# Moved waits in the FFN of a hybrid decoder layer: two late weight loads, two silus, one sum, and the order of the last norms

## Chip, cores and metric

One Trainium2 chip, one core, one launch. The metric is the device time in microseconds (us); the median of several runs is compared. TensorE is called PE, VectorE DVE, ScalarE ACT, GpSimd POOL; SP is the queue that issues all the DMAs named here.

## The reference

One decoder layer over x of 1024 rows by 1024 columns in float32. The first half (three kinds of attention, an output projection, a norm and a residual) is not touched by the change. The second half is

```
h = rms_norm(x, ln_ffn_pre)
f = (silu(h @ ffn_w_gate) * (h @ ffn_w_up)) @ ffn_w_down     # D_FF = 2816
x = x + rms_norm(f, ln_ffn_post)
```

## The kernel before

**Products.** The FFN is written as block products with sums of blocks as operands, seven in place of eight, all of 512 columns. Each float32 operand is cut into a high and a low part, and a product is three matmuls for each block of 128 (high by high, high by low, low by high). The list `seq` (made by `plan_products`) holds 238 products, numbered s. Steps 0 to 155 belong to 22 units u of the gate and up projection with the kinds P1, P2, P6, P7, P5, P3, P4, each of 12 matmuls. The first steps are P1 and P2 of the units 0 to 3 (s = 0 to 7), then P6, P7, P5 of unit 0 (8, 9, 10), P2 of unit 4 (11), P3 and P4 of unit 0 (12, 13), P6 of unit 1 (14). Steps 152, 154 and 156 to 237 are the down projection: three rounds c over 3, 4 and 4 pairs of units, seven kinds D2, D1, D6, D7, D4, D5, D3 in that order, and four output tiles m in each kind. A product of round 0 has 9 matmuls, one of the rounds 1 and 2 has 12. In round 0, D7 has the steps 166 to 169, D5 174 to 177, D3 178 to 181; D2 of round 1 has 182 to 185. D3 of round 2 has 234 to 237, the last.

**Queues.** Every engine runs its instructions strictly in the order written. ACT and DVE walk through the steps s, and at s they cut the stationary operand of step s + 6 (`cut_hi` on ACT, L2057, then `cut_lo` on DVE, L2292). PE waits with step s for its `cut_lo`. ACT copies a half-finished PSUM bank away (`snap_first`, `snap_second` L2070, `snap_third`), and DVE's `first_block(u)` (L2298) adds P2's bank to the copy of P1. `silu_first(u)` (L2078) waits for `first_block(u)`. In `product`, a P2 of unit u from 2 up waits until `first_block(u - 2)` is done, since it takes the same bank: `pe.wait_ge(c11_done, u - 1)`. P5 of unit u waits for `snap_second(u)`, and `snap_second(0)` itself for the last of the ten cuts of the transposed activations (`top_rest`, L2287). `block_sums(1)` is four DVE sums of weights for unit 1, written behind `cut_lo(12)` at step 6. Up to the first steps of the loop, ACT and DVE follow an order written out by hand (called the prologue here).

**Down projection.** DVE makes the sums of the down weights (`down_sums`, L2273 to L2281) at steps from `plan_sums`; ACT (`block_hi_cut`, L2106) and DVE (`block_lo_cut`, L2330) cut them at steps from `plan_blocks`. The cut of the D7 sums stands at steps 162, 163, 164 and the D7 sums at 161, 162, 163. At each step DVE writes: cuts of blocks, then `add_out` (L2325, adds the bank to the running output; a later product that takes the bank waits for it), then `cut_lo(s + 6)`, then sums of weights. SP issues, in the order of a sorted list: `load_acts(q)` (L1890, the activations of round-and-kind q, into `f_stage` for even q and `f_scr` for odd q), `load_late_gate` (L1906, 512 KB each, waits for a D3 sum of the round before), `load_pair_up` (L1898, 512 KB each), the loads for the tail and the stores. q = 6 is D3 of round 0, q = 7 is D2 of round 1.

**Tail.** For an output tile t the class `Finish` has ACT square both halves (`square`, L2615), POOL multiply one half by the gain (`apply_gain`, L2620), and for t from 4 up DVE multiply the other half (`gain_late`, L2628) once that half is squared. ACT makes the mean (L2646), POOL the root (`root`, L2656), DVE the normed residual (`norm`, L2672, both halves; `norm_half`, L2681, one), and SP stores it. They stand behind the last eight `add_out`.

Of the kernel before, what the change touches and what calls it, by code (L numbers as in the profile page):

```python
# [1616 lines left out]
def plan_sums(place):  # L1617


    end, sums = place["P4", UNITS - 1, 0] + 1, []  # L1620
    for k in range(PAIR_SIZES[0]):
        sums += [(end - 1 + k, 0, kind, k) for kind in ("D5", "D6")]
        sums += [(place["D6", 0, 0] - 1 + k, 0, "D7", k), (place["D7", 0, 0] + 2 + k, 0, "D3", k)]
    for c in range(1, PAIR_CHUNKS):
        first = place["D4", c - 1, 0]
        made = [(kind, k) for kind in ("D5", "D6", "D7", "D3") for k in range(PAIR_SIZES[c])]
        sums += [(first + 3 * i // 2, c, kind, k) for i, (kind, k) in enumerate(made)]
    return sorted(sums, key=lambda x: x[0])


def out_and_ffn(nc, core, x, x1, w_gate, w_up, w_pairs, act_pairs, keep, mem, fin):
# [124 lines left out]
    def wait_taken(eng, kind, c, m):  # L1756

        if (kind, c) in COPIED:
            eng.wait_ge(y_copied, copied_at[kind, c, m] + 1)
        else:  # L1760
            eng.wait_ge(y_added, added_at[kind, c, m] + 1)
# [40 lines left out]
    def ahead_of(s):  # L1802

        held = at("P7", 1)
        if s == at("P5", 0):
            return (held, s + AHEAD)
        return (s + AHEAD,) if 3 < s < NS - AHEAD and s + AHEAD != held else ()
# [42 lines left out]
    def sp_program(sp):  # L1850
# [68 lines left out]
        for t in range(NT):  # L1919
# [10 lines left out]
            elif t == NT - 1:  # L1930
# [16 lines left out]
        order += [(NU - 21 if q == 0 else NU - 7.3 if q == 1 else cut_of(q - 2) + 0.7, load_acts, (q,)) for q in range(rounds)]  # L1947
        order += [(at("P5", UNITS - 1) + 0.1 + 0.1 * k if c == 0 else NU + 2 + 0.1 * k if c == 1 else place["D4", c - 2, 0] + 0.1 * k, load_pair_up, (c, k))
                  for c in range(PAIR_CHUNKS) for k in range(PAIR_SIZES[c])]
        order += [(place["D7", c - 1, 0] + 0.1 * k, load_late_gate, (c, k)) for c in range(1, PAIR_CHUNKS) for k in range(PAIR_SIZES[c])]  # L1950
        order += [(place["D1", LAST_ROUND, 0] + 0.1 * t if t < 2 else place["D4", LAST_ROUND, 0] + 0.1 * t, load_last, (t,)) for t in range(NT)]
        for _, what, args in sorted(order, key=lambda job: job[0]):
            what(*args)
        for t in range(NT - 2):
            fin.store(sp, t)
        fin.store_halves(sp, NT - 2)
        fin.store_halves(sp, NT - 1)
        sp.wait_ge(fin.out_done, 16 * (NT + 2))
        for u in range(2):
            sp.wait_ge(x1_out[u], 16 * (NT // 2))  # L1960

# [36 lines left out]
    def act_program(act):  # L1998
# [34 lines left out]
        def top_cut(i):  # L2033
            j, what = TOP_PARTS[i]
            act.wait_ge(y_done, NT)
            act.wait_ge(top_sum, SUMS_AT[j][TOP_NEEDS[what]])
            act.copy(top_part(topH, j, what), top_part(QT, j, what)).then_inc(top_hi, 1)

        def cut_hi(s):
            kind, u, m = seq[s]  # L2040
            if kind in S_STEP:
                act.wait_ge(s_done, 4 * u + S_STEP[kind])
            elif paired(s):
                act.wait_ge(act_in[round_of(s) % 2], acts_in(round_of(s)))
            else:
                wait_raw(act, raw_index(s))
            if s >= W_RING:
                act.wait_ge(prod_done, s - W_RING + 1)
            elif s >= 2:
                act.wait_ge(y_done, NT)  # L2050
                if s >= 5:
                    act.wait_ge(y_normed, NT)
                if s >= 6:
                    act.wait_ge(xn_done, NT)
                if s >= 7:
                    act.wait_ge(xT_done, NT)
            act.copy(slot_part(s, 0), source(s)).then_inc(hi_done, 1)  # L2057

        def snap_first(u):
            act.wait_ge(prod_done, at("P1", u) + 1)  # L2060
            if u >= 3:
                act.wait_ge(a0_done, u - 2)
            elif u == 2:
                act.wait_ge(squares, 2 * NT)
            act.copy(p1_room(u)[:], ps[:, X_BANK[u % 4], :]).then_inc(p1_done, 1)
# [10 lines left out]
        def silu_first(u):  # L2076
            act.wait_ge(c11_done, u + 1)
            act.activation(p1_room(u)[:], p1_room(u)[:], ACT.Silu).then_inc(s11_done, 1)  # L2078
# [52 lines left out]
        block_hi(NT - 1)  # L2131
        top_cut(3)
        snap_first(1)
        top_cut(4)
        cut_hi(6)
        top_cut(5)
        cut_hi(7)
        silu_first(0)
        cut_hi(8)
        top_cut(6)  # L2140
# [2 lines left out]
        cut_hi(9)  # L2143
        top_cut(8)
        top_cut(9)
        silu_first(1)

        for s in range(NS):
            kind, u, m = seq[s]
            for at_step, n in cuts:  # L2150
                if at_step == s:
                    block_hi_cut(n)
            if kind == "P1" and u > FIRST_DRAWN:
                snap_first(u)
            elif kind == "P6":
                snap_second(u)
            elif kind == "P5":
                snap_third(u)
            elif kind == "P3":
                silu_second(u)  # L2160
            elif (kind, u) in COPIED and s >= NU:
                if s == NU:
                    copy_out(place["D2", 0, 0])
                    copy_out(place["D2", 0, 1])
                copy_out(s)
            for v in (3, 4):
                if s == at("P4", v - 3) + 1:
                    snap_first(v)
                elif s == at("P4", v - 3) + 2:
                    silu_first(v)  # L2170
            if s == at("P1", FIRST_DRAWN + 1) + 2:
                silu_first(FIRST_DRAWN + 1)
            if s and seq[s - 1][0] == "P2" and (seq[s - 1][1] == 2 or seq[s - 1][1] > FIRST_DRAWN + 1):
                silu_first(seq[s - 1][1])
            for n in ahead_of(s):
                cut_hi(n)
            if finished(s):
                if finished(s) == (0, 0):
                    wait_up_read(act, LAST_ROUND - 1)
                wait_taken(act, kind, u, m)  # L2180
                fin.square(act, *finished(s))
                if finished(s)[0] >= M_PAIRS and finished(s)[1] == 0:
                    fin.mean(act, finished(s)[0])

    def dve_program(dve):
# [108 lines left out]
        def first_block(u):  # L2294

            dve.wait_ge(prod_done, at("P2", u) + 1)
            dve.wait_ge(p1_done, u + 1)
            dve.tensor_tensor(p1_room(u)[:], ps[:, Y_BANK[u % 2], :], p1_room(u)[:], ALU.add).then_inc(c11_done, 1)  # L2298
# [84 lines left out]
        for s in range(NS):  # L2383
            kind, u, m = seq[s]
            for at_step, n in cuts:
                if at_step == s:
                    block_lo_cut(n)
            if s and seq[s - 1][0] == "P5":
                last_block(seq[s - 1][1])
            for v in (3, 4):  # L2390
                if s == at("P4", v - 3) + 1:
                    first_block(v)
            if s == at("P1", FIRST_DRAWN + 1) + 1:
                first_block(FIRST_DRAWN + 1)
            if kind == "P2" and (u == 2 or u > FIRST_DRAWN + 1):
                first_block(u)
            if s and seq[s - 1][0] == "P3":
                late_half(seq[s - 1][1])
            if kind == "P4":
                early_half(u)  # L2400
            if paired(s) and (kind, u) not in COPIED:
                add_out(s)
            for n in ahead_of(s):
                cut_lo(n)
                if seq[n][0] == "P3" and seq[n][1] + 1 < UNITS:
                    block_sums(seq[n][1] + 1)
            for at_step, *item in sum_plan:
                if at_step == s:
                    down_sums(*item)
            if paired(s) and u == LAST_ROUND:  # L2410
                n = s - place["D5", LAST_ROUND, 0]
                if n == 0:
                    fin.first_means(dve)
                elif 1 <= n < 4:
                    fin.norm(dve, n - 1)
                elif n == 4:
                    fin.half_means(dve)
                    wait_taken(dve, *seq[s])
                    fin.gain_late(dve, 4)
                    fin.norm(dve, 3)  # L2420
                elif n in (5, 6):
                    wait_taken(dve, *seq[s])
                    fin.gain_late(dve, n)
                    fin.norm(dve, n - 1)
                    if n == 6:
                        fin.norm_half(dve, 6, 1)
        fin.norm_half(dve, NT - 2, 0)
        wait_taken(dve, *seq[NS - 1])
        fin.gain_late(dve, NT - 1)
        fin.norm_half(dve, NT - 1, 1)  # L2430
# [127 lines left out]
class Finish:  # L2558
# [42 lines left out]
    def store_halves(self, sp, t):  # L2601
        for n, i in enumerate((1, 0)):
            cols = slice(i * HALF, (i + 1) * HALF)
            sp.wait_ge(self.sum_done, t + (t == NT - 1) + 1 + n)
            sp.dma_start(self.out[t * P:(t + 1) * P, cols], self.room(t)[:, cols]).then_inc(self.out_done, 16)

    def constants(self, pool):
# [231 lines left out]
```

## Time and profile before

| | |
|---|---|
| median of 3 runs | 1252.41 us (1250.11 to 1258.15) |
| the profiled execution | 1252.77 us, span 1251.0 us |
| PE busy | 1217.7 us, 97% |
| DVE busy | 866.4 us, 69% |
| ACT busy | 605.7 us, 48% |
| POOL busy | 181.4 us, 15% |
| mean granted clock of PE | 0.993 |
| 640 to 1000 us | PE busy 360.00 us with 1590 matmuls, 0.226 us each; 12 of them take 2.7 us, 9 take 2.04 |
| busy share of the DMA engines | 0.00 from 626 to 640 us; 0.00 from 1059 to 1062; 0.62 from 1062 to 1067; 0.86 from 1067 to 1083 |

Times in the rows are us from the span's start. In a timeline row the first number is the start, the second the busy time, and a bracket tells how long the engine was idle just before and what released it. Rows of one engine lie a little over each other, so the pace is read from start to start: on DVE 0.60 us for an operation whose busy time is 0.69, and 1.20 for one of 1.28. "issue" is a wait that the profile ascribes to nothing.

### The profile page before, as it was taken

Reading aid. Unit: us, or ns where it says so; the run is one execution under the profiler, and the core shown is the slowest. Engines: PE = TensorE matmul, PEld = TensorE weight load, DVE = VectorE, ACT = ScalarE, POOL = GpSimd, SP = SyncE. Lnnn points to the kernel's source line nnn. Section 1 sums busy time; section 2 is a strip of 40 time slices with the busy share of each in tenths; the row PEclk is TensorE's granted clock in tenths of the full one; section 3 lists DMA queues with packets and bytes.
Section 4 is the critical chain, followed back from the end, with each engine's and each line's share of the span. In section 5 each row is a group of like instructions: output and inputs, shape, how many; then the busy total and the mean of one; then the engine's idle time right before and its main releaser. Section 6 shows DMA issues by size and latency. Waiting matters only on the chain.

```text
span 1251.0 us, 18763 instructions
## 1 busy us (share of the span) xinstructions
PE 1217.7 (97%) x6592; PEld 1042.2 (83%) x6592; DVE 866.4 (69%) x1641; ACT 605.7 (48%) x1167; POOL 181.4 (15%) x153
## 2 busy tenths in 40 slices
PE   9999999999999999999989999999999999999996
PEld 7898878888988999888878888888888888788885
DVE  6323788858878665355876657667666568897888
ACT  5432677657776566344653333333333345444343
POOL 5230111111000000011001112112122021000114
PEclk9999999999999999999999999999999999999998
DMA  6303511136842100222312232333332455743443
GB/s 234 120 1 119 118 37 49 35 110 158 182 121 77 26 18 18 68 101 100 119 42 100 94 125 67 103 127 103 108 105 72 144 193 195 259 156 115 151 169 135
DMA packets 66881, 136.93 MB, mean 109 GB/s; under 512 B 8503, under 2 KB 27199, under 8 KB 66788
## 3 DMA queue, kind: packets, MB, share of 16 engines
q1 hardware_dynamic: 66788, 135.74, 34.0%
q8 instruction: 53, 0.87, 0.3%
q14 instruction: 40, 0.33, 0.1%
HBM read 90.33 MB, written 28.60 MB: 95 GB/s over the span
## 4 chain that ended last, share of the span: by engine, by line
PE 79%; DVE 9%; issue 5%; ACT 3%; DMA 2%; SPq 1%; DVEq 0%; POOL 0%; ACTq 0%; POOLq 0%
PE ps L2506 32%; PE ps L2536 11%; PE ps L1097 7%; PE ps L2450 6%; PE ps L941 4%; PE ps L1077 4%; PE ps L886 3%; PE ps L960 3%; PE ps L1042 2%; PE ps L1050 2%; DVE ring L1468 2%; PE ps L975 1%; DMA m_qs<-m_qn 1%; DVE ring L1460 1%; DVE QT L2325 1%
## 5 line engine op out<-in xcount | busy, mean ns | idle before, releaser
L2506 PE MATMUL ps<-f_topH,f_W 128*128 128x512 f32 x704 | 221.0, 389 | 3.8 <-DVE f_W L2292 2.1
L2506 PEld LDWEIGHTS ps<-f_topH,f_W 128*128 128x128 f32 x704 | 132.1, 188 | 32.0 <-DVE f_W L2292 4.6
L2292 DVE TENSOR_TENSOR f_W<-f_scr,f_W 128x512 fp32r<-128x512 f32 (+1 forms) x128 | 89.9, 705 | 84.9 <-ACT f_W L2057 84.8
L2506 PE MATMUL ps<-f_topL,f_W 128*128 128x512 f32 x352 | 136.9, 389 | 0.0
L1097 PE MATMUL ps<-V,m_tw 128*128 128x66 f32 (+1 forms) x1056 | 129.2, 273 | 2.3 <-DVE m_mix_n L1518 2.2
L1097 PEld LDWEIGHTS ps<-V,m_tw 128*128 128x128 f32 x1056 | 126.3, 193 | 5.3 <-DVE m_mix_n L1518 4.3
L2536 PE MATMUL ps<-f_headH,f_W 128*128 128x512 f32 x408 | 128.0, 390 | 2.2 <-issue 1.5
L2506 PE MATMUL ps<-f_headH,f_W 128*128 128x512 f32 x352 | 114.7, 390 | 0.0
L2536 PEld LDWEIGHTS ps<-f_headH,f_W 128*128 128x128 f32 x408 | 76.6, 188 | 19.6 <-issue 2.7
L2057 ACT CAST f_W<-f_scr 128x512 fp32r<-128x512 f32 (+1 forms) x128 | 77.6, 610 | 24.6 <-PE ps L2536 15.2
L2292 DVE TENSOR_TENSOR f_W<-ring,f_W 128x512 fp32r<-128x512 f32 x60 | 59.6, 1006 | 33.4 <-ACT f_W L2057 33.3
L1277 ACT COPY m_tw<-ps 128x512 f32<-128x512 f32 (+1 forms) x101 | 56.5, 568 | 52.0 <-PE ps L1097 29.8
L2536 PE MATMUL ps<-f_headL,f_W 128*128 128x512 f32 x204 | 79.4, 389 | 0.0
L2506 PEld LDWEIGHTS ps<-f_topL,f_W 128*128 128x128 f32 x352 | 66.1, 188 | 13.7
L2506 PEld LDWEIGHTS ps<-f_headH,f_W 128*128 128x128 f32 x352 | 66.1, 188 | 13.6
L2506 PE MATMUL ps<-f_headL,f_W 128*128 128x512 f32 x176 | 68.5, 389 | 0.0
L960 PE MATMUL ps<-m_hH,m_wH 128*128 128x512 f32 x144 | 60.4, 419 | 4.9 <-ACT QT L1178 4.8
L2536 PE MATMUL ps<-f_b22H,f_W 128*128 128x512 f32 x208 | 65.1, 389 | 0.0
L2450 PE MATMUL ps<-o_w,o_mH 128*128 128x512 f32 x224 | 60.5, 392 | 0.0
L2506 PE MATMUL ps<-f_b22H,f_W 128*128 128x512 f32 x176 | 57.8, 389 | 0.0
L2325 DVE TENSOR_TENSOR QT<-ps,QT 128x512 f32<-128x512 f32 x68 | 46.7, 687 | 15.7 <-PE ps L2536 15.7
L1042 PE MATMUL ps<-m_KSa,m_qs 128*128 128x256 f32 (+7 forms) x168 | 55.0, 345 | 2.3 <-DVE m_rows_sb L1475 1.2
(279 smaller groups left out, 2660.4 us busy)
## 6 DMA issues: line engine op xcount, KB each, us to landing
act_pairs<-QT SPq DMA_DIRECT2D x77, 256.0 KB, 4.1
m_qs<-m_qn SPq DMA_DIRECT2D x128, 128.0 KB, 2.4
ring<-in_ffn_w_up SPq DMA_DIRECT2D x22, 512.0 KB, 3.7
f_stage<-act_pairs SPq DMA_DIRECT2D x40, 256.0 KB, 3.6
ring<-in_ffn_w_gate SPq DMA_DIRECT2D x19, 512.0 KB, 4.5
f_scr<-act_pairs SPq DMA_DIRECT2D x37, 256.0 KB, 3.1
ring<-in_ffn_w_down SPq DMA_DIRECT2D x11, 512.0 KB, 5.3
f_pair_up<-in_ffn_w_down SPq DMA_DIRECT2D x11, 512.0 KB, 6.6
```

The source lines that it names most:

```text
L941: ins = pe.matmul(ps[:, b + a, 0:VW_HALF], h[:, k, tok], wv[:, w, k, a * VW_HALF:(a + 1) * VW_HALF], start=(k == 0 and h is hH and w == 0) ...
L960: ins = pe.matmul(ps[:, bank, :], w[:, n % W_ITEMS, cols], a[:, k, hf * HALF:(hf + 1) * HALF], start=(k == 0 and w is wH and a is hH), sto ...
L1042: pe.matmul(out, q_hi_, k, start=True, stop=False)
L1077: ins = pe.transpose(ps[:, bank, i * P:(i + 1) * P], rows, ident[:])
L1097: ins = pe.matmul(ps[:, SUMS, wide * i:wide * (i + 1)], tw[:, t % W_SLOTS, P * i:P * i + P], v, start=(kb == 0 and i == 0), stop=(kb == jo ...
L1277: act.copy(out, src).then_inc(kept_by["act"], 1)
L2057: act.copy(slot_part(s, 0), source(s)).then_inc(hi_done, 1)
L2292: dve.tensor_tensor(slot_part(s, 1), source(s), slot_part(s, 0).bitcast(F32), ALU.subtract).then_inc(lo_done, 1)
L2325: dve.tensor_tensor(part, product_, part, ALU.add).then_inc(y_added, 1)
L2450: ins = pe.matmul(ps[:, 2 * (t % 2) + hf, :], m[:, t % 2, k, :], w[k][:, a, hf * HALF:(hf + 1) * HALF], start=(k == 0 and m is mH and a == ...
L2506: ins = pe.matmul(ps[:, bank, :], whole[:, w, cols], halves[h][:, k0 + k, col:col + HALF], start=(begins and k == 0 and w == 0 and h == 0) ...
L2536: ins = pe.matmul(ps[:, bank, :], whole[:, w, k * P:(k + 1) * P], block(n)[h], start=(begins and k == 0 and w == 0 and h == 0), stop=(k == ...
```

## The change

It has five edits. (1) `load_late_gate` of round 1 moves behind `load_acts(6)` in SP's order. (2) In ACT's prologue `cut_hi(6)` and `cut_hi(7)` move ahead of `top_cut(4)`; `silu_first(1)` leaves the end of the prologue and `silu_first(2)` its place at step 6, and both now follow `snap_second(0)` at step 8. (3) On DVE `first_block(2)` moves from step 5 to step 8, behind `cut_lo(13)` and ahead of `cut_lo(14)`. (4) The D7 sums of round 0 are made one step earlier. (5) In the tail the steps 234, 235 and 236 run `norm` of the tile before and then `gain_late` of their own, without waiting in between; tile 6 is normed and stored whole, not in halves.

```diff
-        sums += [(place["D6", 0, 0] - 1 + k, 0, "D7", k), (place["D7", 0, 0] + 2 + k, 0, "D3", k)]
+        sums += [(place["D6", 0, 0] - 2 + k, 0, "D7", k), (place["D7", 0, 0] + 2 + k, 0, "D3", k)]
...
-        order += [(place["D7", c - 1, 0] + 0.1 * k, load_late_gate, (c, k)) for c in range(1, PAIR_CHUNKS) for k in range(PAIR_SIZES[c])]
+        order += [(place["D7", c - 1, 0] + 0.1 * k + (1.8 if c == 1 else 0), load_late_gate, (c, k)) for c in range(1, PAIR_CHUNKS) for k in range(PAIR_SIZES[c])]
...
-        for t in range(NT - 2):
+        for t in range(NT - 1):
             fin.store(sp, t)
-        fin.store_halves(sp, NT - 2)
         fin.store_halves(sp, NT - 1)
...
         snap_first(1)
+        cut_hi(6)
+        cut_hi(7)
         top_cut(4)
-        cut_hi(6)
         top_cut(5)
-        cut_hi(7)
         silu_first(0)
...
         top_cut(9)
-        silu_first(1)
...
-            if s and seq[s - 1][0] == "P2" and (seq[s - 1][1] == 2 or seq[s - 1][1] > FIRST_DRAWN + 1):
+            if s and seq[s - 1][0] == "P2" and seq[s - 1][1] > FIRST_DRAWN + 1:
                 silu_first(seq[s - 1][1])
+            if s == at("P6", 0):
+                silu_first(1)
+                silu_first(2)
...
-            if kind == "P2" and (u == 2 or u > FIRST_DRAWN + 1):
-                first_block(u)
+            if s == at("P6", 0) or kind == "P2" and u > FIRST_DRAWN + 1:
+                first_block(2 if kind == "P6" else u)
...
-                elif n == 4:
-                    fin.half_means(dve)
-                    wait_taken(dve, *seq[s])
-                    fin.gain_late(dve, 4)
-                    fin.norm(dve, 3)
-                elif n in (5, 6):
-                    wait_taken(dve, *seq[s])
-                    fin.gain_late(dve, n)
-                    fin.norm(dve, n - 1)
-                    if n == 6:
-                        fin.norm_half(dve, 6, 1)
-        fin.norm_half(dve, NT - 2, 0)
+                elif n >= 4:
+                    if n == 4:
+                        fin.half_means(dve)
+                    if n < 7:
+                        fin.norm(dve, n - 1)
+                        fin.gain_late(dve, n)
+        fin.norm(dve, NT - 2)
```

## Rows read from the trace of the kernel before

**Rows 1.** Who waited for whom, PE from 560 to 1251: total, times, longest us

```profile
PE ps L2506 <- DVE f_W L2292: 2.1, 1, 2.1
PE ps L2506 <- ACT QT L2070: 1.7, 1, 1.7
PE ps L2536 <- issue: 1.5, 1, 1.5
PE ps L2536 <- DVE f_headL L2330: 0.6, 1, 0.6
```

**Rows 2.** Timeline of PE, the first matmuls of P7, P5 and P2(4)

```profile
631.51 0.50 PE L2506 MATMUL ps<-f_topH,f_W 128*128 128x512 f32 x1 [2.13 <-DVE f_W L2292]
...
636.18 0.47 PE L2506 MATMUL ps<-f_topH,f_W 128*128 128x512 f32 x1 [1.66 <-ACT QT L2070]
...
639.02 0.39 PE L2506 MATMUL ps<-f_headH,f_W 128*128 128x512 f32 x1
```

**Rows 3.** Timeline of DVE: cut_lo 7 and 9, first_block(2), cut_lo 12 and 13

```profile
622.54 0.69 DVE L2292 TENSOR_TENSOR f_W<-f_gates,f_W 128x512 fp32r<-128x512 f32 x1 [0.66 <-ACT f_W L2057]
...
630.77 0.69 DVE L2292 TENSOR_TENSOR f_W<-f_scr,f_W 128x512 fp32r<-128x512 f32 x1
...
633.18 0.69 DVE L2298 TENSOR_TENSOR f_p1b<-ps,f_p1b 128x512 f32<-128x512 f32 x1
...
635.07 0.69 DVE L2292 TENSOR_TENSOR f_W<-f_scr,f_W 128x512 fp32r<-128x512 f32 x1 [0.60 <-ACT f_W L2057]
...
638.43 0.69 DVE L2292 TENSOR_TENSOR f_W<-ring,f_W 128x512 fp32r<-128x512 f32 x1
```

**Rows 4.** Timeline of ACT: cut_hi(6) and cut_hi(7)

```profile
619.32 0.62 ACT L2057 CAST f_W<-f_gates 128x512 fp32r<-128x512 f32 x1
...
621.89 0.62 ACT L2057 CAST f_W<-f_gates 128x512 fp32r<-128x512 f32 x1
```

**Rows 5.** Timeline of DVE: the third D7 cut, then add_out of step 174

```profile
1053.87 0.69 DVE L2330 TENSOR_TENSOR f_headL<-f_down_sums,f_headH 128x512 fp32r<-128x512 f32 x1 [0.69 <-ACT f_headH L2106]
...
1078.78 0.68 DVE L2325 TENSOR_TENSOR QT<-ps,QT 128x512 f32<-128x512 f32 x1
```

**Rows 6.** Timeline of PE: start of step 178, and the last matmul

```profile
1079.56 0.47 PE L2536 MATMUL ps<-f_headH,f_W 128*128 128x512 f32 x1 [1.49 <-issue]
...
1240.53 0.39 PE L2536 MATMUL ps<-f_b22H,f_W 128*128 128x512 f32 x1
```

**Rows 7.** Timeline of ACT: cut_hi(178) and cut_hi(182)

```profile
1075.43 0.51 ACT L2057 CAST f_W<-f_stage 128x384 fp32r<-128x384 f32 x1 [10.26 <-DMA f_stage<-act_pairs]
...
1082.97 0.62 ACT L2057 CAST f_W<-f_scr 128x512 fp32r<-128x512 f32 x1 [4.23 <-DMA f_scr<-act_pairs]
```

**Rows 8.** Timeline of SP's issues: late gates, acts 6, acts 7

```profile
1062.01 5.12 SPq L1906 DMA_DIRECT2D ring<-in_ffn_w_down  x4
1067.24 1.79 SPq L1890 DMA_DIRECT2D f_stage<-act_pairs  x3
...
1071.57 2.29 SPq L1890 DMA_DIRECT2D f_scr<-act_pairs  x4
```

**Rows 9.** Timeline of DVE in the tail: add_out(234), gain_late(5), add_out(237), the last halves

```profile
1233.89 0.68 DVE L2325 TENSOR_TENSOR QT<-ps,QT 128x512 f32<-128x512 f32 x1
...
1238.83 0.69 DVE L2628 TENSOR_TENSOR QT<-QT,e_last_gain 128x512 f32<-128x512 f32 x1 [0.89 <-ACT e_last_junk L2615]
...
1244.68 0.68 DVE L2325 TENSOR_TENSOR QT<-ps,QT 128x512 f32<-128x512 f32 x1
...
1247.10 0.75 DVE L2681 SCALAR_TENSOR_TENSOR e_xt_sums<-QT,e_rs,e_xt_sums 128x512 f32<-128x512 f32 x1 [0.48 <-POOL e_rs L2656]
1247.77 0.75 DVE L2681 SCALAR_TENSOR_TENSOR e_xt_sums<-e_gained_last,e_rs,e_xt_sums 128x512 f32<-128x512 f32 x1
```

**Rows 10.** By line: norm L2672 and root L2656, duration ns min/median/max, first to last

```profile
L2672 DVE SCALAR_TENSOR_TENSOR e_xt_up<-QT,e_rs,e_xt_up x4: 1277/1280/1714, 1232.3 to 1242.8; 128x1024 f32<-128x1024 f32 x4
...
L2656 POOL TENSOR_TENSOR e_rs<-e_ms,e_mhalf x4: 544/818/823, 1235.7 to 1246.5; 128x1 f32<-128x1 f32 x4
```

More of the change, by code:

```diff
@@ L1953, in sp_program @@
             what(*args)
-        for t in range(NT - 2):
+        for t in range(NT - 1):
             fin.store(sp, t)
-        fin.store_halves(sp, NT - 2)
         fin.store_halves(sp, NT - 1)
-        sp.wait_ge(fin.out_done, 16 * (NT + 2))
+        sp.wait_ge(fin.out_done, 16 * (NT + 1))
         for u in range(2):
@@ L2603, in store_halves @@
             cols = slice(i * HALF, (i + 1) * HALF)
-            sp.wait_ge(self.sum_done, t + (t == NT - 1) + 1 + n)
+            sp.wait_ge(self.sum_done, t + 1 + n)
             sp.dma_start(self.out[t * P:(t + 1) * P, cols], self.room(t)[:, cols]).then_inc(self.out_done, 16)
```

## The prediction, made before the changed kernel had run

> **What bounds the kernel now.** I read the busy shares first: PE works 97% of the span, so up to its end only PE's own pauses can be won. Then I read who PE waited for from the FFN on: four waits and no fifth, 2.1 + 1.7 + 1.5 + 0.6 = 5.9 us [rows 1]. Placing each in the timeline, the first two are P7 and P5 of unit 0 [rows 2], the one of 0.6 is the first D7 product of round 0, and the "issue" one is step 178, the first D3 product of round 0 [rows 6]. Last I read what follows PE's end: the last matmul is over at 1240.53 + 0.39 = 1240.9 [rows 6] and the span at 1251.0, so 10.1 us of tail hang on DVE. The change removes no matmul. It can win at most the pauses and a part of the tail.
>
> **Prologue and unit 0 (edits 2 and 3).** P7 waited for `cut_lo(9)`, which DVE reached at 630.77 [rows 3]. DVE had been busy since it waited 0.66 for the high part of weight 7 [rows 3], and that came late because ACT made it at 621.89, behind the top cuts; cut straight behind number 6, at 619.32 + 0.5, it is ready by 620.5 [rows 4]. So the 0.66 goes, `cut_lo(9)` starts at 630.1, and P7 at 630.85 instead of 631.51. Edit 2 costs no new work: cuts and silus are as many as before. The wait for weight 9 that is left, 2.13 - 0.66 = 1.5, is DVE being full.
>
> P5 waited until 636.18 for `snap_second(0)` [rows 2], which ACT reached late, behind two silus and four cuts. Without the silus it waits only for the last top cuts, some 1.8 us behind `cut_lo(9)`: about 632.0 for DVE and 632.5 for ACT. P7 takes 2.73 us, so P5 could start at 630.85 + 2.8 = 633.6, and its wait of 1.66 is gone.
>
> But look what is late next. P2 of unit 4 is the product behind P5 and waits for `first_block(2)`. Before, that ran at 633.18 [rows 3] and was long done. Now it stands behind `cut_lo(12)`, the four sums of `block_sums(1)` and `cut_lo(13)`. From `cut_lo(12)` to `cut_lo(13)` DVE took 638.43 - 635.07 = 3.36 us [rows 3], all of it those sums. In the new order `cut_lo(11)` takes the place of `first_block(2)`, 633.18 - 0.66 = 632.5; `cut_lo(12)` follows at 633.1 (ACT, rid of the silus, no longer keeps it waiting 0.60), `cut_lo(13)` at 636.5, `first_block(2)` at 637.1 to 637.8. P5 would let P2(4) start at 633.6 + 2.75 = 636.35. So a wait of about 1.4 us appears there, and P2(4) starts at 637.8 instead of 639.02 [rows 2]. **Gain 1.2 us**. If DVE also saves 0.2 in the handover of weight 6, it is 1.4. I take 1.3. The ends: 0 if the sums take longer, and 639.02 - 636.35 = 2.7 if `first_block(2)` isn't late. Behind the moved silus ACT holds `cut_hi(14)` and `snap_third(0)` until 638.4; step 14 is due three products (8 us) after step 11, and P3, which wants `snap_third(0)`, one product after it at 640.5. Both are covered.
>
> **D7 sums (edit 4).** D7 waited 0.6 for its third low cut, 1053.87 + 0.69 [rows 5]. There the two engines pass one step to and fro: ACT cuts a sum, copies a bank, cuts a weight; DVE cuts its low part, makes the next sum, and only that lets ACT go on (DVE idle 0.69 for ACT). With the sum made a step sooner ACT waits for none of them; it follows PE, and the third cut comes a product (2.04 us) sooner, against a need of 0.6. The sum of 0.60 now stands ahead of an `add_out` that is wanted 4 us later: nothing. **Gain 0.8**, the 0.63 idle and the slower first matmuls after a pause (0.50 instead of 0.39). Ends 0 and 0.8.
>
> **SP order (edit 1).** Step 178 seems to wait for nothing, but DVE's `add_out(174)` ran at 1078.78 [rows 5], and 178 uses its bank: 1079.46 against 1079.56 [rows 6]. DVE was late because `cut_lo(178)`, written ahead of it, waited for ACT, and ACT sat 10.26 us for `load_acts(6)` [rows 7]. SP issued that at 1067.24 behind four late gates that occupied it from 1062.01 [rows 8]. These wait for D3 sums, `load_acts(6)` only for `cut_lo(173)`, which ended at about 1059.4. In the new order it is issued there, while the DMA engines have nothing to do, and has 15 us. The late gates can't be issued before 1062.0 anyway, and `load_acts(6)` takes 1.8 us of SP: moving behind it costs them nothing. What is late next is `load_acts(7)`, for which ACT sat until 1082.97 [rows 7]. SP is free of 1.8 us ahead of it (1071.57 to about 1069.7 [rows 8]) and 0.75 MB less is queued, so it should land at about 1081. The `add_out` of step 177 stands 2.5 us behind `cut_hi(182)` and is wanted by step 181, at 1077.9 + 3 x 2.04 = 1084.0: just in time. **Gain 1.8**: the 1.49, the slow restart and about 0.2 of small gaps behind it. Ends: 0.8 if step 181 waits a microsecond, 2.1 if all small gaps go too.
>
> **Tail (edit 5).** DVE is the engine to follow from 1233.89 [rows 9]. Its work from there is four `add_out`, one small mean, four `norm`, four `gain_late` and two last halves (tile 6 in halves costs 0.1 more). It waited 0.89 for the square ahead of `gain_late(5)`, as much ahead of `gain_late(6)`, 0.3 ahead of `gain_late(4)`, and 0.48 for the last root [rows 9]; the first three waits came from `gain_late(n)` standing straight behind `add_out(n)`. In the new order a `norm`, paced at 1.20 us [rows 10], lies between, and square, mean and root fit beside the DVE work of one step (0.6 + 1.2 + 0.6 = 2.4 us). From 1233.89 `add_out(237)` then has ahead of it three `add_out`, the mean, three `norm` and three gains: 3 x 0.60 + 0.6 + 3 x 1.20 + 3 x 0.60 = 7.8, so it starts at 1241.7 (PE is done at 1240.9, so not earlier for PE's sake) instead of 1244.68. From there square, mean and root of tile 7 took 1247.10 - 1244.68 = 2.4 us with a root of 0.54; other roots took 0.82 [rows 10], so 2.4 to 2.7, and the first of the last halves starts at 1244.1 to 1244.4 instead of 1247.10. `norm(6)` and the last gain (1.8) fit inside. The last two halves and their store come as before. Storing tile 6 whole puts 512 KB on the queue 1 us ahead of them; it was the same bytes before. **Gain 2.7**, ends 1.5 and 3.0.
>
> The roots are where a page speaks against this. The last root took 0.54 us beside an idle DVE, the others up to 0.82 beside a busy one, and the slowest `norm` of the group 1.71 beside POOL's gains, against 1.28 [rows 10]. The Trainium skill, "SBUF — State Buffer", section "SBUF: two separate sides", says that a DVE operation with two SBUF inputs and a GpSimd operation that reads SBUF exclude each other for a whole instruction. The rows agree in direction. By that rule a root could sit out a whole `norm` now that DVE has no pauses, which would take 1.2 from the tail's gain.
>
> **Sum.** 1.3 + 0.8 + 1.8 + 2.7 = 6.6 us against the profiled execution's 1252.77 (span 1251.0 and 1.8 around it): 1246.2. That execution lies 0.4 above the median of 1252.41, far inside the runs' spread of 8 us, so I leave it: **1246.2 us**.
>
> **Rivals.**
> (a) `first_block(2)` is not late, everything comes at its upper end: 2.7 + 0.8 + 2.1 + 3.0 = 8.6, 1244.2. For it: both big waits of unit 0 are named by the profile. Against: the 3.36 us of sums. Chance 0.15.
> (b) The waits move instead of going: the roots sit out a `norm` (tail 1.5), step 181 waits (0.8), unit 0 gives 0.5: 3.6, 1249.2. Chance 0.20.
> (c) The change does nothing that can be seen, the time falls in the runs' own spread: 1251 to 1254. It needs PE to be paced by something that I don't see; the long stretches of full PE speak against it. Chance 0.08.
> (d) Slower: `first_block(2)` at step 8. Every microsecond that it comes after 637.8 is one on PE, as P2(4), then P3 and P4 wait in line. It turns unit 0 to a loss from 639.0 on, and the whole change only after 637.8 + 6.6 = 644.4, that is, if `block_sums(1)` took three times its 3.36 us, say, waiting for its weights. At 10 us more it gives 1256. Against: the DMA engines moved nothing from 626 to 640 us, so those weights had landed. Chance 0.05; by over 1%, 0.02.
> The forecast itself, 1245 to 1248: 0.52.
>
> **Range and chances.** 1243.0 to 1251.0 holds (a), the forecast and (b), and leaves out most of (c) and (d). Over 1% (12.5 us, about what a measurement of this kernel can tell from no change) is more than all four waits and the gain in the tail together, so "faster" gets 0.03, "slower" 0.02 and "same" 0.95.
>
> **What would show it.** P7 of unit 0 starts near 630.9 with some 1.5 us idle, P5 without a wait, P2(4) near 637.8 behind a wait for DVE L2298. No wait at the first D7 and D3 product of round 0; ACT idle far under 10 us at `cut_hi(178)`. `add_out(237)` about 0.9 us behind the last matmul instead of 3.8. I am wrong on unit 0 if P2(4) doesn't wait, on SP's order if step 181 or 182 waits over 1 us for `f_scr`, and on the tail if DVE idles for POOL ahead of a `norm`.

## The result and the profile after

The changed kernel took **1246.23 us** (median of 9 runs, 1244.60 to 1248.10), the kernel before 1251.46 us in 9 runs beside them (1248.59 to 1258.15): **ratio 0.995, 95% interval 0.9932 to 0.9968**. A second session gave 0.994 (0.9927 to 0.9952). The profiled execution took 1246.82 us with a span of 1245.0, against 1252.77 and 1251.0. No work went: PE still runs 6592 matmuls.

Who waited for whom, PE from 560 us to the end, in the changed kernel (total, times, longest). Two waits are left where [rows 1] had four, and one of them is new:

```profile
PE ps L2502 <- DVE f_p1b L2299: 1.3, 1, 1.3
PE ps L2502 <- DVE f_W L2293: 1.3, 1, 1.3
```

Lines have moved by a few: PE's products are L2502 and L2532 now, `cut_lo` L2293, `first_block` L2299, `add_out` L2326, `cut_hi` L2056, `norm` L2668, `root` L2652.

Timeline of PE: the first FFN matmul, P7, P2 of unit 4, step 178 and the last matmul, which answer to [rows 2, 6].

```profile
604.65 0.48 PE L2502 MATMUL ps<-f_headH,f_W 128*128 128x512 f32 x1
...
631.57 0.50 PE L2502 MATMUL ps<-f_topH,f_W 128*128 128x512 f32 x1 [1.29 <-DVE f_W L2293]
...
638.63 0.47 PE L2502 MATMUL ps<-f_headH,f_W 128*128 128x512 f32 x1 [1.33 <-DVE f_p1b L2299]
...
1076.64 0.39 PE L2532 MATMUL ps<-f_headH,f_W 128*128 128x512 f32 x1
...
1237.10 0.39 PE L2532 MATMUL ps<-f_b22H,f_W 128*128 128x512 f32 x1
```

P5 is not in the list of waits: its 1.66 is gone. But `first_block(2)` now keeps P2(4) waiting 1.33. Absolute times mislead here. The FFN began at 604.65 in this execution and at 603.75 in that of before, in code that is the same in both, so each stretch has to be read from its own start:

| stretch | before | after | gain | predicted |
|---|---|---|---|---|
| first FFN matmul to P2(4) | 35.27 | 33.98 | 1.29 | 1.3 |
| P2(4) to the last matmul's start | 601.51 | 598.47 | 3.04 | 0.8 + 1.8 |
| last matmul's start to the end | 10.47 | 7.90 | 2.57 | 2.7 |
| sum of the three | 647.25 | 640.35 | 6.90 | 6.6 |
| start of the span to the first FFN matmul | 603.75 | 604.65 | -0.90 | 0 |

Timeline of DVE: `cut_lo(9)`, `cut_lo(12)`, `cut_lo(13)`, `first_block(2)`, which answer to [rows 3].

```profile
630.84 0.68 DVE L2293 TENSOR_TENSOR f_W<-f_scr,f_W 128x512 fp32r<-128x512 f32 x1
...
633.85 0.68 DVE L2293 TENSOR_TENSOR f_W<-f_scr,f_W 128x512 fp32r<-128x512 f32 x1
...
637.20 0.69 DVE L2293 TENSOR_TENSOR f_W<-ring,f_W 128x512 fp32r<-128x512 f32 x1
637.80 0.68 DVE L2299 TENSOR_TENSOR f_p1b<-ps,f_p1b 128x512 f32<-128x512 f32 x1
```

From 633.85 to 637.20, 3.35 us pass with `cut_lo(12)` and the four sums, as 3.36 before; `first_block(2)` ends at 638.48 and P2(4) starts at 638.63.

SP's issues (`load_acts(6)`, late gates, `load_pair_up`, `load_acts(7)`), which answer to [rows 8], and then ACT's `cut_hi(178)` and `cut_hi(182)`, which answer to [rows 7]:

```profile
1058.06 1.27 SPq L1890 DMA_DIRECT2D f_stage<-act_pairs  x3
1060.75 5.31 SPq L1906 DMA_DIRECT2D ring<-in_ffn_w_down  x4
1066.18 2.35 SPq L1898 DMA_DIRECT2D f_pair_up<-in_ffn_w_down  x4
1068.62 2.43 SPq L1890 DMA_DIRECT2D f_scr<-act_pairs  x4
```

```profile
1063.81 0.51 ACT L2056 CAST f_W<-f_stage 128x384 fp32r<-128x384 f32 x1
...
1079.55 0.62 ACT L2056 CAST f_W<-f_scr 128x512 fp32r<-128x512 f32 x1 [9.25 <-DMA f_scr<-act_pairs]
```

`cut_hi(178)` no longer waits. ACT's long pause has only moved: it now sits 9.25 us at `cut_hi(182)`, the next load (4.23 before), where little hangs on it. Idle time of ACT is not PE's.

Timeline of DVE in the tail: `add_out` of 234 and 237 and the two last halves, which answer to [rows 9]; then the root by line (ns min/median/max), which answers to [rows 10].

```profile
1230.47 0.68 DVE L2326 TENSOR_TENSOR QT<-ps,QT 128x512 f32<-128x512 f32 x1
...
1238.24 0.68 DVE L2326 TENSOR_TENSOR QT<-ps,QT 128x512 f32<-128x512 f32 x1
...
1241.15 0.75 DVE L2677 SCALAR_TENSOR_TENSOR e_xt_sums<-QT,e_rs,e_xt_sums 128x512 f32<-128x512 f32 x1 [0.44 <-POOL e_rs L2652]
1241.82 0.75 DVE L2677 SCALAR_TENSOR_TENSOR e_xt_sums<-e_gained_last,e_rs,e_xt_sums 128x512 f32<-128x512 f32 x1
```

```profile
L2652 POOL TENSOR_TENSOR e_rs<-e_ms,e_mhalf x4: 1011/1034/1037, 1232.3 to 1240.1; 128x1 f32<-128x1 f32 x4
```

From `add_out(234)` to `add_out(237)` DVE takes 7.77 us (7.8 predicted, 10.79 before) and never waits. All four roots take 1.01 to 1.04 us where they took 0.54 to 0.82.

### The profile page after: what moved, and what is told of

Its sections match the earlier page's. It is cut to its first block, busy times and chain, and to the rows that moved or that the text cites. A ratio compares the mean times of both kernels' runs of the same rounds, so it can differ in the third digit from the quotient of the medians.

```text
span 1245.0 us, 18759 instructions
## 1 busy us (share of the span) xinstructions
PE 1218.6 (98%) x6592; PEld 1044.3 (84%) x6592; DVE 864.8 (69%) x1640; ACT 605.6 (49%) x1167; POOL 182.1 (15%) x153
## 4 chain that ended last, share of the span: by engine, by line
PE 79%; DVE 10%; issue 4%; ACT 3%; DMA 2%; POOL 1%; SPq 1%; DVEq 0%; POOLq 0%; ACTq 0%
PE ps L2502 31%; PE ps L2532 14%; PE ps L1097 7%; PE ps L2446 4%; PE ps L941 4%; PE ps L1077 4%; PE ps L886 4%; PE ps L960 3%; PE ps L1042 2%; PE ps L1050 2%; DVE ring L1468 2%; PE ps L975 1%; DMA m_qs<-m_qn 1%; DVE ring L1460 1%; DVE m_rows_sb L1475 1%
## 5 line engine op out<-in xcount | busy, mean ns | idle before, releaser
L2502 PE MATMUL ps<-f_topH,f_W 128*128 128x512 f32 x704 | 220.7, 389 | 1.3 <-DVE f_W L2293 1.3
L2502 PEld LDWEIGHTS ps<-f_topH,f_W 128*128 128x128 f32 x704 | 132.1, 188 | 29.0 <-DVE f_W L2293 1.7
L2293 DVE TENSOR_TENSOR f_W<-f_scr,f_W 128x512 fp32r<-128x512 f32 (+1 forms) x128 | 89.8, 704 | 87.8 <-ACT f_W L2056 87.7
L2502 PE MATMUL ps<-f_topL,f_W 128*128 128x512 f32 x352 | 136.9, 389 | 0.0
L2532 PE MATMUL ps<-f_headH,f_W 128*128 128x512 f32 x408 | 127.3, 389 | 0.0
L2502 PE MATMUL ps<-f_headH,f_W 128*128 128x512 f32 x352 | 114.8, 390 | 1.3 <-DVE f_p1b L2299 1.3
L2056 ACT CAST f_W<-f_scr 128x512 fp32r<-128x512 f32 (+1 forms) x128 | 77.6, 610 | 27.5 <-PE ps L2532 15.1
L2532 PEld LDWEIGHTS ps<-f_headH,f_W 128*128 128x128 f32 x408 | 76.6, 188 | 16.3 <-issue 0.3
L2293 DVE TENSOR_TENSOR f_W<-ring,f_W 128x512 fp32r<-128x512 f32 x60 | 59.6, 1006 | 33.4 <-ACT f_W L2056 33.3
L2532 PE MATMUL ps<-f_headL,f_W 128*128 128x512 f32 x204 | 79.4, 389 | 0.0
L2502 PEld LDWEIGHTS ps<-f_headH,f_W 128*128 128x128 f32 x352 | 66.1, 188 | 15.3 <-DVE f_W L2293 1.7
L2502 PEld LDWEIGHTS ps<-f_topL,f_W 128*128 128x128 f32 x352 | 66.1, 188 | 13.8
L2502 PE MATMUL ps<-f_headL,f_W 128*128 128x512 f32 x176 | 68.5, 389 | 0.0
L2532 PE MATMUL ps<-f_b22H,f_W 128*128 128x512 f32 x208 | 65.2, 389 | 0.0
L2502 PE MATMUL ps<-f_b22H,f_W 128*128 128x512 f32 x176 | 57.7, 389 | 0.0
L2326 DVE TENSOR_TENSOR QT<-ps,QT 128x512 f32<-128x512 f32 x68 | 46.6, 685 | 15.8 <-PE ps L2532 15.8
```

Source lines behind the costliest of these rows:

```text
L2293: dve.tensor_tensor(slot_part(s, 1), source(s), slot_part(s, 0).bitcast(F32), ALU.subtract).then_inc(lo_done, 1)
L2502: ins = pe.matmul(ps[:, bank, :], whole[:, w, cols], halves[h][:, k0 + k, col:col + HALF], start=(begins and k == 0 and w == 0 and h == 0) ...
L2532: ins = pe.matmul(ps[:, bank, :], whole[:, w, k * P:(k + 1) * P], block(n)[h], start=(begins and k == 0 and w == 0 and h == 0), stop=(k == ...
```

## The experiments

All but the last two are single executions: they are told apart by stretches of the profile, not by the time of the whole. Each starts from the changed kernel. The columns: start of the first FFN matmul in the span; from there to P2(4); from P2(4) to the last matmul's start; from there to the end; span.

| kernel | FFN starts | to P2(4) | to last | tail | span |
|---|---|---|---|---|---|
| before | 603.75 | 35.27 | 601.51 | 10.47 | 1251.0 |
| changed | 604.65 | 33.98 | 598.47 | 7.90 | 1245.0 |
| block_early | 605.15 | 32.58 | 598.64 | 7.93 | 1244.3 |
| cuts_old | 603.29 | 34.82 | 598.67 | 7.92 | 1244.7 |
| split_sums | 605.71 | 33.27 | 598.21 | 7.91 | 1245.1 |
| sp_old | 601.42 | 34.05 | 600.63 | 7.90 | 1244.0 |
| d7_old | 606.99 | 34.16 | 599.23 | 7.92 | 1248.3 |
| tail_wait | 605.41 | 34.11 | 598.29 | 10.29 | 1248.1 |
| root_free | 601.89 | 33.95 | 598.68 | 8.38 | 1242.9 |
| tail_add_first | 606.02 | 33.92 | 598.30 | 7.96 | 1246.2 |

Where no edit touches a stretch, the rows differ by up to 0.24 us to P2(4), 0.47 from there to the last matmul and 0.03 in the tail; what is read as an effect lies above that. The spans would mislead: sp_old undoes a part of the change and has a smaller span than the changed kernel, because its FFN began 3.2 us sooner.

**block_early: is it `first_block(2)`?**

```diff
-            if s == at("P6", 0) or kind == "P2" and u > FIRST_DRAWN + 1:
-                first_block(2 if kind == "P6" else u)
+            if s == at("P1", 3) or kind == "P2" and u > FIRST_DRAWN + 1:
+                first_block(2 if kind == "P1" else u)
```

> Changed kernel, with first_block(2) moved to step 6, ahead of cut_lo(12) and the four sums of block_sums(1); the silus stay behind snap_second(0). My theory: P2 of unit 4 waits (1.33 us in the changed kernel) only because first_block(2) stands behind those sums. Then that wait is gone and P2(4) starts 1.3 to 1.5 us sooner after the first FFN matmul, 32.5 to 32.7 us instead of 33.98; P7 still waits 1.3. Rival: P2(4) is held by its own weight cut or by ACT, which sits in silu_first(2); then the wait stays at about 1.3 under another name.

P2(4) came at 32.58, 1.40 sooner, and its wait is gone. PE's timeline, P7 and P2(4):

```profile
632.14 0.50 PE L2502 MATMUL ps<-f_topH,f_W 128*128 128x512 f32 x1 [1.36 <-DVE f_W L2293]
...
637.73 0.39 PE L2502 MATMUL ps<-f_headH,f_W 128*128 128x512 f32 x1
```

That shows the place behind the sums to be the cause; the rival falls.

**cuts_old: what do the earlier cuts give?**

```diff
         snap_first(1)
-        cut_hi(6)
-        cut_hi(7)
         top_cut(4)
+        cut_hi(6)
         top_cut(5)
+        cut_hi(7)
```

> Changed kernel, with cut_hi(6) and cut_hi(7) back behind top_cut(4) and top_cut(5) on ACT. My theory: DVE is a full chain from weight 6 to first_block(2), and the 0.7 to 0.9 us that the earlier cuts gave runs through to P2(4): P7 starts 0.7 to 0.9 later (its wait is 2.0 to 2.2 instead of 1.3 to 1.4) and P2(4) starts at 34.6 to 34.9 us after the first FFN matmul instead of 33.98. Rival: P2(4) is paced by the sums' own waits, so only P7 moves, and P2(4) stays at 34.0.

P7's wait went from 1.29 to 2.13, and P2(4) came 0.84 later, with the same wait of its own. The two rows:

```profile
631.05 0.50 PE L2502 MATMUL ps<-f_topH,f_W 128*128 128x512 f32 x1 [2.13 <-DVE f_W L2293]
...
638.11 0.47 PE L2502 MATMUL ps<-f_headH,f_W 128*128 128x512 f32 x1 [1.33 <-DVE f_p1b L2299]
```

So DVE is one full chain from weight 6 to `first_block(2)`. Of the 1.29 us, 0.84 come from the cuts. The other 0.45 is what a subtraction leaves for the moved silus and `first_block(2)` together; no run put these two back, and rows of this stretch differ by 0.24. The place of `first_block(2)` alone gives away the 1.40 that block_early wins.

**split_sums: can P7's wait go too?**

```diff
-        sums(2, (2,))
-        sums(3, (2,))
+        sums(2, (3,))
+        sums(3, (3,))
         top_rest(6)
         top_rest(7)
         cut_lo(9)
+        sums(2, (4,))
+        sums(3, (4,))
+        cut_lo(10)
         top_rest(8)
...
         cut_hi(9)
+        cut_hi(10)
         top_cut(8)
```

Part 3 is the first of the two sums of part 2 and part 4 the second, with the counts that wait for them renumbered; `ahead_of` leaves out product 10. `first_block(2)` stands as in block_early.

> Changed kernel with first_block(2) at step 6 (as in block_early), and two of DVE's top sums, which only the last two top cuts need, moved behind cut_lo(9); cut_hi(10) and cut_lo(10) go ahead of those last top cuts. Theory: the 1.3 us that P7 still waits are DVE being full, and 1.2 us of it isn't needed by P7. Then P7 waits 0.1 to 0.3 us, P5 waits at most 0.6 for snap_second(0), and P2(4) starts 31.3 to 31.9 us after the first FFN matmul (32.58 in block_early, 33.98 in the changed kernel). Rival: the pause moves whole to P5, which needs those last top cuts by way of snap_second(0), and P2(4) stays at 32.6.

A miss: P2(4) at 33.27, later than the theory and the rival have it and 0.69 later than in block_early, though still 0.71 sooner than in the changed kernel. P7's wait fell only to 0.76, since the top cuts 6 and 7 on ACT now kept DVE waiting 0.57, and P5 got one of 1.03 for `snap_second(0)`, which the delayed top cuts and three weight cuts on ACT held up:

```profile
632.10 0.50 PE L2507 MATMUL ps<-f_topH,f_W 128*128 128x512 f32 x1 [0.76 <-DVE f_W L2295]
...
636.14 0.47 PE L2507 MATMUL ps<-f_topH,f_W 128*128 128x512 f32 x1 [1.03 <-ACT QT L2069]
```

P7's pause shrank by 0.60, and P5's new one is longer than that: 0.76 + 1.03 = 1.79 us where block_early has one wait of 1.36. The rival was nearer.

**sp_old: the order of two loads.**

```diff
-        order += [(place["D7", c - 1, 0] + 0.1 * k + (1.8 if c == 1 else 0), load_late_gate, (c, k)) for c in range(1, PAIR_CHUNKS) for k in range(PAIR_SIZES[c])]
+        order += [(place["D7", c - 1, 0] + 0.1 * k, load_late_gate, (c, k)) for c in range(1, PAIR_CHUNKS) for k in range(PAIR_SIZES[c])]
```

> Changed kernel, with the four late gates of round 1 back ahead of load_acts(6). My theory: the wait is made by the order in SP's queue. Then ACT sits some 10 us for f_stage again, add_out(174) comes late, and PE waits 1.3 to 1.7 us at step 178 under the name issue. Rival: the wait of before came from the D7 pause and the backlog it left on ACT and DVE, which is gone; then ACT waits for f_stage but PE shows no wait at step 178, and the stretch from P2(4) to the last matmul stays at 598.5 us.

P2(4) to the last matmul took 600.63, 2.16 more. ACT's row for `cut_hi(178)`, and PE's for step 178:

```profile
1070.98 0.51 ACT L2056 CAST f_W<-f_stage 128x384 fp32r<-128x384 f32 x1 [10.20 <-DMA f_stage<-act_pairs]
```

```profile
1075.11 0.47 PE L2532 MATMUL ps<-f_headH,f_W 128*128 128x512 f32 x1 [1.44 <-issue]
```

Here the D7 pause was absent and the wait came all the same: the order in SP's queue makes it. Behind it PE also starts the steps 179 and 181 late, by 0.25 and 0.29 us (0.25 and 0.27 in the kernel before); these gaps are too short for the list of waits.

**d7_old: the D7 sums one step later.**

```diff
-        sums += [(place["D6", 0, 0] - 2 + k, 0, "D7", k), (place["D7", 0, 0] + 2 + k, 0, "D3", k)]
+        sums += [(place["D6", 0, 0] - 1 + k, 0, "D7", k), (place["D7", 0, 0] + 2 + k, 0, "D3", k)]
```

> Changed kernel, with the D7 sums of round 0 back at the steps 161 to 163. My theory: ACT and DVE pass one step to and fro, so PE waits 0.5 to 0.7 us for the third D7 cut (DVE L2331) and that is all: P2(4) to the last matmul takes 0.8 us more than 598.5. Rival: with the other waits gone DVE has enough lead and no wait shows.

599.23, 0.76 more, with PE's wait of 0.6 (the first line) and the old rhythm of the D7 cuts on DVE, 2.75 us apart with 0.69 of waiting in each. In the changed kernel they are 1.67 and 1.07 apart, and the third one, at 1050.65, ends 2.2 us ahead of the matmul that needs it.

```profile
PE ps L2532 <- DVE f_headL L2331: 0.6, 1, 0.6
```

```profile
1053.34 0.69 DVE L2331 TENSOR_TENSOR f_headL<-f_down_sums,f_headH 128x512 fp32r<-128x512 f32 x1 [0.69 <-ACT f_headH L2105]
1056.08 0.69 DVE L2331 TENSOR_TENSOR f_headL<-f_down_sums,f_headH 128x512 fp32r<-128x512 f32 x1 [0.69 <-ACT f_headH L2105]
```

**tail_wait: the order of DVE or the whole tile?**

```diff
-                elif n >= 4:
+                elif n in (4, 5, 6):
                     if n == 4:
                         fin.half_means(dve)
-                    if n < 7:
-                        fin.norm(dve, n - 1)
-                        fin.gain_late(dve, n)
+                    wait_taken(dve, *seq[s])
+                    fin.gain_late(dve, n)
+                    fin.norm(dve, n - 1)
```

> Changed kernel, with gain_late(n) back straight behind add_out(n), ahead of norm(n-1), at the steps 234 to 236; tile 6 is still normed and stored whole. My theory: the order of DVE is the tail's gain. Then DVE waits 0.3, 0.9, 0.9 us for the squares again and from the last matmul's start to the end it takes 10.0 to 10.4 us instead of 7.9. Rival: the gain is the whole store and whole norm of tile 6; then it stays within 0.5 of 7.9.

10.29 us, with the three waits back (0.30 and twice 0.89):

```profile
1236.14 0.69 DVE L2624 TENSOR_TENSOR QT<-QT,e_last_gain 128x512 f32<-128x512 f32 x1 [0.89 <-ACT e_last_junk L2611]
...
1239.52 0.69 DVE L2624 TENSOR_TENSOR QT<-QT,e_last_gain 128x512 f32<-128x512 f32 x1 [0.89 <-ACT e_last_junk L2611]
```

So 2.39 of the tail's 2.57 us are the order. The 0.18 that is left goes, by subtraction, to the whole tile in place of two halves.

**root_free: who holds the root?**

```diff
-        fin.gain_late(dve, NT - 1)
         fin.norm_half(dve, NT - 1, 1)
+        fin.gain_late(dve, NT - 1)
         fin.norm_half(dve, NT - 1, 0)
...
         dve.wait_ge(self.rs_done, t - M_PAIRS + 2)
-        self.wait_gained(dve, t)
+        if i == 1:
+            dve.wait_ge(self.gained, 2 * M_PAIRS + t - M_PAIRS + 1)
+        else:
+            self.wait_gained(dve, t)
```

> Changed kernel, with the last gain on DVE (gain_late(7)) between the two last halves, so that DVE stands idle behind norm(6) while POOL makes the root of tile 7. It tests whether POOL's root is held by DVE's operation beside it. The roots took 1.01 to 1.04 us in the changed kernel, 0.54 for the one root of before beside an idle DVE. Theory (a root waits until DVE's operation with two SBUF inputs is over): the last root takes 0.5 to 0.65 us and the first last half starts 0.4 to 0.5 sooner after add_out(237) (2.9 us in the changed kernel), while the end stays within 0.2. Rival (the root simply takes 1.0 us when another operation of the queue precedes it closely): it still takes 1.0.

POOL's last two roots, the first beside a busy DVE and the second beside an idle one:

```profile
1235.10 1.03 POOL L2652 TENSOR_TENSOR e_rs<-e_ms,e_mhalf 128x1 f32<-128x1 f32 x1 [1.36 <-ACT e_ms L2642]
1237.49 0.55 POOL L2652 TENSOR_TENSOR e_rs<-e_ms,e_mhalf 128x1 f32<-128x1 f32 x1 [1.36 <-ACT e_ms L2642]
```

DVE's two last halves in the same kernel, with the gain between them:

```profile
1238.12 0.75 DVE L2680 SCALAR_TENSOR_TENSOR e_xt_sums<-QT,e_rs,e_xt_sums 128x512 f32<-128x512 f32 x1 [0.60 <-issue]
1238.79 0.68 DVE L2621 TENSOR_TENSOR e_gained_last<-QT,e_last_gain 128x512 f32<-128x512 f32 x1
1239.68 0.75 DVE L2680 SCALAR_TENSOR_TENSOR e_xt_sums<-e_gained_last,e_rs,e_xt_sums 128x512 f32<-128x512 f32 x1 [0.20 <-DVE e_gained_last L2621]
```

The root takes 0.55 us, and the first half starts 2.47 us behind `add_out(237)` instead of 2.91, as the theory has it. The end was missed: the gain now stands between the halves, with 0.20 of waiting for its own result behind it, and the tail is 8.38, 0.48 longer.

**tail_add_first: `add_out(237)` sooner.**

```diff
                     if n < 7:
                         fin.norm(dve, n - 1)
-                        fin.gain_late(dve, n)
+                    if n < 6:
+                        fin.gain_late(dve, n)
+                    elif n == 7:
+                        fin.gain_late(dve, 6)
```

> Changed kernel, with gain_late(6) behind add_out(237) instead of ahead of it. Theory: the tail is now the chain add_out(237), square, mean, root, two halves, and DVE has 0.44 us to spare inside it; add_out(237) 0.6 us sooner makes the tail 0.4 to 0.6 us shorter, 7.3 to 7.5 us from the last matmul's start to the end instead of 7.90. Rival: DVE's own work is the limit, nothing is won.

Nothing won: 7.96. `add_out(237)` did start 0.59 us sooner behind the last matmul. The rival has the reason: DVE's own work sets the end. Two waits of 0.20 for DVE's own results were added (`norm(6)` behind its gain, the first last half behind the last gain). The root now began inside `norm(6)` and took 1.32 us, but it was over at 1241.94, 0.41 us before the half that needs it started. DVE's `add_out(237)` and `norm(6)`, then POOL's last two roots:

```profile
1238.79 0.68 DVE L2326 TENSOR_TENSOR QT<-ps,QT 128x512 f32<-128x512 f32 x1
...
1240.26 1.28 DVE L2671 SCALAR_TENSOR_TENSOR e_xt_sums<-QT,e_rs,e_xt_sums 128x1024 f32<-128x1024 f32 x1 [0.20 <-DVE QT L2627]
```

```profile
1238.83 0.54 POOL L2655 TENSOR_TENSOR e_rs<-e_ms,e_mhalf 128x1 f32<-128x1 f32 x1 [1.36 <-ACT e_ms L2645]
1240.62 1.32 POOL L2655 TENSOR_TENSOR e_rs<-e_ms,e_mhalf 128x1 f32<-128x1 f32 x1 [1.25 <-ACT e_ms L2645]
```

These rows say what a root costs. By the pace of 1.20 us `norm(6)` ran until 1241.46, 0.84 us after the second root had begun, and the root took 0.48 more than that. The last root of the changed kernel fits the same sum: it began at 1240.08, 0.56 us before a gain was over, and took 1.04. So do the roots of 0.82 before, with 0.33 to 0.34 of a gain left. Over the twelve traces 45 of the 48 roots of the tiles 4 to 7 take 0.47 to 0.50 us more than the DVE operation beside them has left. Two others began when DVE's operation was over or within 0.02 us of its end, and took 0.55 and 0.54. The last one is the first root shown here: it began beside `add_out(237)`, with 0.56 us of it left, and took 0.54 all the same. That operation is as long as a gain but reads one of its two inputs from a PSUM bank (`ps`), where the gain and the `norm` read both from SBUF. So, as far as these traces show, a root sits out the rest of a DVE operation with two inputs in SBUF, and a DVE that is merely busy doesn't hold it; of the second half there is only this one case.

**block_early_timed and after_again.** The kernel of block_early and the changed kernel, both against the kernel before on one chip.

> The kernel of block_early, timed. By the stretches of the first look the part behind the first FFN matmul takes 639.2 us against 640.4 in the changed kernel and 647.3 in the one before. Theory: 1.2 us of PE's wait are gone for good, so it stands 8.1 us below the kernel before (ratio 0.9935) and 1.2 below the changed kernel. Rival: the start of the first FFN matmul, which moved between 601.4 and 607.0 us from execution to execution in code that no kernel here touches, covers the 1.2 us, and the two can't be told apart by their times.

> The changed kernel once more, on the same chip as block_early_timed. Expected ratio to the kernel before 0.994 to 0.996 (0.995 was measured). Its profile should again show two waits of PE in the FFN, 1.2 to 1.4 us each, and a tail of 7.9 us, with the first FFN matmul anywhere between 601 and 607 us and sooner where the granted clock of the first 600 us is higher.

block_early: 1243.19 us (1240.93 to 1244.72, 5 runs), before 1251.82 (9 runs), ratio 0.9935 (0.9921 to 0.9948). Changed kernel: 1243.72 us (1243.36 to 1245.53, 5 runs), ratio 0.994 (0.9927 to 0.9952). The FFN stretches took 638.92 and 640.21 us in their profiles, so the 1.3 us is there, and the changed kernel shows its two waits (1.34 and 1.33) and a tail of 7.89 again. Both ratios came as expected. But the medians of the two kernels lie 0.5 us apart and not 1.2, and the intervals overlap: as the rival has it, by the times alone block_early isn't shown to be faster than the changed kernel.

## Why the prediction was right

**Unit 0**: right in each step. P7's wait shrank (1.5 predicted, 1.29 measured), P5's vanished, and P2(4) got a new one of 1.33 (1.4 predicted) behind `first_block(2)`. The gain of 1.29 is what is left when one takes the two waits that vanish or shrink and looks for what is late next. Without a late `first_block(2)` the prediction had 2.7, its upper end, and block_early, where it isn't late, gives exactly that (35.27 - 32.58 = 2.69). The DVE handover that I priced at 0.66, with up to 0.2 more, gave 0.84. One reading was loose: the 3.36 us from `cut_lo(12)` to `cut_lo(13)` are not all sums. About 0.8 are `cut_lo(12)` itself and a short gap, and the four sums take 2.54; the forecast counted from start to start, so it doesn't suffer.

**D7 sums**: 0.8 predicted, 0.76 by d7_old. That ACT waits for none of these sums was nearly right: for the second and the third it still waits 0.15 us each, where it had been 1.23.

**SP order**: the mechanism was right and the term too small: 1.8 predicted, 2.16 by sp_old, 3.04 - 0.76 = 2.3 by the stretch. What I had too small were the gaps behind step 178: about 0.2 us in my sum, 0.25 at step 179 and 0.29 at step 181 in sp_old. (Rows of this stretch differ by 0.47 where nothing is edited, so the last tenths are not to be read.) `load_acts(7)` was in by 1079.55, 2.9 us behind the start of step 178 (1081 against 1077.9, 3.1 us, predicted), and left one gap of 0.15 us at step 181, the "just in time" of the prediction. block_early shows the same place once with 0.18.

**Tail**: 2.7 predicted, 2.57 measured. DVE's sum of work was right to 0.03 us. The part behind it was not: from `add_out(237)` to the first last half I allowed 2.4 to 2.7 us and it took 2.91, since the root took 1.04. The Trainium skill's rule of the shared port ("SBUF — State Buffer", section "SBUF: two separate sides") is what tail_add_first shows: the root waits for the rest of a DVE operation with two inputs in SBUF. The price I drew from it, a whole `norm` of 1.2, was too high for this order: the last root began beside a gain that had 0.56 us left. The price in my sum, a root of 0.54 to 0.82, was too low. The rival (b) falls, since the tail gave 2.57 and not 1.5, and (c) and (d) with the stretches.

**The median**: 1246.23 against 1246.2 is luck in the last digit. The stretches gained 6.9 and the FFN began 0.9 later, so the profiled execution fell by 5.95 and not by 6.6. The two medians differ by 5.2 us in one session and by 8.1 in the other.

## What to carry to other kernels

Price a removed wait by the next thing that is late, not by its own length: walk down the in-order queue of the engine that had been waited for, count what now stands ahead of each result, and compare it with the time when PE will ask for it. When an engine waits for a transfer and "issue" appears elsewhere, look at which load stands in the queue behind loads that wait for later events, and put first what is wanted first. For a short POOL operation, look at what DVE is doing when it begins, and add what is left of that operation where both of its inputs lie in SBUF. With gains of some tenths of a per cent, compare stretches of the profile from a common mark, since the rest of the program moves by more than the effect.

## What the runs showed that I had not expected

The first FFN matmul began anywhere from 600.18 to 606.99 us, in code that is the same in all these kernels: a spread of 6.8 us, as much as the whole change gives, while the part behind it repeats within about 0.3. A part of it seems to lie with PE's granted clock. In root_free (FFN at 601.89) it was at its upper level, 2.4 GHz, in each of the two stretches below (1.00); in d7_old (FFN at 606.99) the mean was 0.94 and 0.93, so for a part of them it was at the lower, 1.2 GHz, though PE was about as busy there (29.77 us against 29.91, and 48.41 against 48.42). Columns: stretch; us, PE, PEld, DVE, ACT and POOL busy; granted clock; DMA share; GB/s. root_free first:

```profile
30.00:60.00 30.00, 29.91 (x162) 25.66 (x161) 12.61 (x15) 14.18 (x24) 7.61 (x4) 1.00 0.38 125
...
400.00:450.00 50.00, 48.42 (x356) 42.81 (x355) 36.03 (x153) 30.59 (x54) 1.62 (x3) 1.00 0.17 43
```

Then d7_old:

```profile
30.00:60.00 30.00, 29.77 (x153) 25.82 (x152) 12.62 (x15) 13.43 (x22) 6.91 (x4) 0.94 0.41 125
...
400.00:450.00 50.00, 48.41 (x357) 45.19 (x357) 35.92 (x144) 28.64 (x53) 1.62 (x3) 0.93 0.13 33
```

In all twelve traces the clock from 400 to 450 us goes with the start of the FFN: the three with 1.00 began it at 600.18 to 601.89, the six with 0.93 at 603.29 to 606.99. The three with 0.97 lie anywhere: sp_old at 601.42, block_early at 605.15, split_sums at 605.71, all with 0.94 from 30 to 60 us. So the clock isn't all of it, and what sets it from run to run stays open; no experiment was made on it.
